# Two heads in one matmul of 128 rows in the recurrent levels of a hybrid decoder trunk

## The reference

```
logf = logaddexp(log(lb), log1p(-lb) + log_sigmoid(f));  k = -expm1(logf);  q = silu(q_raw)
b = cumsum(logf)                                   # along the tokens of a chunk
attn[t, s] = sum_c q[t, c] * exp(b[t, c] - b[s, c]) * k[s, c]     for s <= t
o = attn @ v + (q * exp(b)) @ state
```

## Time and profile before

| | |
|---|---|
| median of three runs | 2279.16 us (2278.46 to 2280.85) |
| profiled execution, its own time | 2280.71 us |
| its span | 2278.9 us |
| PE, DVE, ACT, POOL busy | 94%, 65%, 44%, 17% |
| mean granted TensorE clock | 0.983 of 2.4 GHz |
| levels stage, layer 1 | 164.5 to 280.5 us |
| levels stage, layer 2 | 1287.3 to 1402.7 us |

### The profile page before, as it was taken

The page is one execution under the profiler, slowest core; times in us unless marked ns, Lnnn a source line. Parts: engine busy times, 40 slices in busy tenths (PEclk is TensorE's granted clock), DMA queues, the critical chain, the costliest instruction groups (busy, mean ns, idle before and its releaser), DMA issues.

```text
span 2278.9 us, 32746 instructions
## 1 busy us (share of the span) xinstructions
PE 2146.6 (94%) x12051; PEld 1714.9 (75%) x12051; DVE 1486.5 (65%) x2695; ACT 1009.7 (44%) x1867; POOL 377.5 (17%) x346
## 2 busy tenths in 40 slices
PE   7999999999899998999999999999998989999996
PEld 4897788777677786777579878887866878777774
DVE  4637776654667876777656486766265678377775
ACT  4523334543465335555434233345344643345552
POOL 2002200000000341344300121000000014124441
PEclk9999999999999999999999999999999999999998
DMA  9322333331225675776542223423222266546753
GB/s 309 93 86 61 94 101 93 103 92 51 80 78 175 243 245 226 284 250 247 190 153 85 76 79 93 130 79 93 79 61 79 79 226 241 201 167 247 256 211 119
DMA packets 196573, 333.71 MB, mean 146 GB/s; under 512 B 30528, under 2 KB 153280, under 8 KB 180416
## 3 DMA queue, kind: packets, MB, share of 16 engines
q1 hardware_dynamic: 169184, 305.33, 39.6%
q0 software_dynamic: 19296, 19.98, 2.8%
q10 hardware_dynamic: 7936, 6.30, 0.8%
HBM read 352.48 MB, written 51.38 MB: 177 GB/s over the span
## 4 chain that ended last, share of the span: by engine, by line
PE 73%; DVE 13%; ACT 6%; issue 3%; DMA 3%; POOL 0%; SPq 0%; POOLq 0%; ACTq 0%; DVEq 0%
PE ps L874 68%; PE ps L872 5%; DVE spare L2077 2%; DVE ring_rounded L2095 2%; ACT WH_rounded L1587 2%; DVE nmax L2323 1%; DVE ssq L2262 1%; DMA SQKV<-gate_logits 1%; DMA DVt<-gate_logits 1%; DVE ps L2320 1%; DMA Y<-y_rows 1%; DVE DQK L2264 0%; DVE SC L2693 0%; ACT SC L1723 0%; POOL M L3035 0%
## 5 line engine op out<-in xcount | busy, mean ns | idle before, releaser
L874 PE MATMUL ps<-X_rounded,WH_rounded 128*128 128x512 f32 x768 | 343.8, 448 | 20.9 <-ACT CM L1635 6.5
L2095 DVE TENSOR_TENSOR ring_rounded<-ring,WH_rounded 128x512 fp32r<-128x512 f32 (+2 forms) x190 | 234.9, 1245 | 134.7 <-ACT WH_rounded L1587 134.3
L874 PE MATMUL ps<-H_rounded,WH_rounded 128*128 128x512 f32 x768 | 304.4, 396 | 8.9 <-DVE SC L2693 8.9
L874 PE MATMUL ps<-X_rounded,ring_rounded 128*128 128x512 f32 x768 | 304.3, 396 | 0.0
L874 PE MATMUL ps<-WH_rounded,X_rounded 128*128 128x256 f32 (+1 forms) x960 | 275.1, 287 | 3.1 <-ACT M L1868 1.0
L874 PE MATMUL ps<-ring_rounded,X_rounded 128*128 128x256 f32 (+1 forms) x960 | 271.5, 283 | 0.0
L874 PE MATMUL ps<-WH_rounded,H_rounded 128*128 128x256 f32 (+1 forms) x960 | 271.4, 283 | 0.0
L3035 POOL TENSOR_TENSOR M<-M,SC 128x512 f32<-128x512 f32 x48 | 75.8, 1591 | 997.9 <-DVE SC L2693 997.9
L1587 ACT ACTIVATE WH_rounded<-ring 128x512 fp32r<-128x512 f32 (+2 forms) x190 | 195.2, 1037 | 70.6 <-PE ps L874 62.3
L874 PEld LDWEIGHTS ps<-X_rounded,WH_rounded 128*128 128x128 f32 x768 | 146.7, 191 | 76.4 <-issue 30.4
L874 PEld LDWEIGHTS ps<-WH_rounded,X_rounded 128*128 128x128 f32 x960 | 184.8, 192 | 5.3 <-issue 2.4
(11 more groups left out here) (399 smaller groups left out, 4503.5 us busy)
## 6 DMA issues: line engine op xcount, KB each, us to landing
ring<-in_w_in SPq DMA_DIRECT2D x272, 256.0 KB, 3.9
Y<-in_moe_w_down SPq DMA_DIRECT2D x18, 1024.0 KB, 6.6
ring<-in_ada_w SPq DMA_DIRECT2D x64, 256.0 KB, 4.7
ring<-in_w_branch SPq DMA_DIRECT2D x64, 256.0 KB, 5.4
TM<-in_ada_w SPq DMA_DIRECT2D x14, 1024.0 KB, 10.2
DQK<-in_ada_w SPq DMA_DIRECT2D x14, 1024.0 KB, 9.4
ring<-in_moe_w_down SPq DMA_DIRECT2D x14, 1024.0 KB, 6.4
gate_logits<-CM SPq DMA_DIRECT2D x44, 256.0 KB, 2.9
```

The source lines that it names most:

```text
L874: ins = nc.tensor.matmul(o, lhsT, rhs, start=start, stop=stop)
L2095: ins = v.tensor_tensor(low[j][:, at:at + size], ring[:, j, at:at + size], high[i][:, at:at + size].bitcast(F32), ALU.subtract)
```

## The change

At levels 1 to 7 both heads go through one matmul. The queries are laid out for each token block as two groups of 64 columns, one a head, with zeros in the other head's 64 partitions. A matmul then takes 128 rows and 128 columns, four instead of eight a level, and writes both heads into one PSUM bank (4 or 1, by the level's parity).

The zeros come out of the exponentials: ACT writes the query factors into a new buffer `hgEq` (in DVt, cleared once a layer), each head's partitions into its own group of columns. The one exponential over 128 x 512 becomes three: the early half (128 x 256, with scale -1), and the late half once for each head (64 x 256). POOL multiplies the whole late half of the queries by each of the two groups: two multiplications of 128 x 256 instead of one, and `qs_ready` counts two. On DVE `decay` is one difference over all 512 columns instead of two over 256, and `keep` one predicated copy of 512 columns instead of two of 256. Level 0, step 8, the key product and the order of the queues stay.

```diff
@@ TensorE, levels
-                        eng.wait_ge(qs_ready[i], p.next(qs_ready[i]))
+                        eng.wait_ge(qs_ready[i], p.next(qs_ready[i], 2))
                         eng.wait_ge(ks_ready[i], p.next(ks_ready[i]))
+                        b = level_bank(lv)
+                        free(b)
+                        for c in range(NT):
+                            ins = mm(level_out(b)[:, :, c], hgKs[i][:, tt(c)], hgQs[i][:, c], last=c == 3)
+                        ins.then_inc(filled[b], p.gives(filled[b]))
-                                ins = mm(ps[:, b, c * HD:(c + 1) * HD], k[r, tt(c)], half(q[r, tt(c)], lv, 1), last=last)
@@ ACT
-                            act(hgE[i], hgE[i], ACT.Exp).then_inc(e_ready[i], p.gives(e_ready[i]))
+                                keys_of, late = (half(hgE[i], j, side) for side in range(2))
+                                act(keys_of, keys_of, ACT.Exp, scale=-1.0)
+                                for side in range(2):
+                                    r = slice(side * HD, (side + 1) * HD)
+                                    ins = act(hgEq[i][r, :, side].rearrange("p c (n h) -> p c n h", h=1 << j >> 1),
+                                              late[r].rearrange("p (c n) h -> p c n h", c=NT), ACT.Exp)
+                                ins.then_inc(e_ready[i], p.gives(e_ready[i]))
@@ DVE, decay and keep
-                    v.tensor_tensor(half(hgE[i], j, 0), ref, first, ALU.subtract)
-                    v.tensor_tensor(half(hgE[i], j, 1), second, ref, ALU.subtract).then_inc(
+                    v.tensor_tensor(hgE[i].rearrange("p (n s) -> p n s", s=size), spans, ref, ALU.subtract).then_inc(
...
+                    both = DQK[:, pr % 2, :].rearrange("p (c n a h) -> p c n a h", c=2 * NT, a=2, h=h)[:, :, :, 1]
+                    v.copy_predicated(both, mask.unsqueeze(1).to_broadcast([P, 2 * NT, n, h]),
+                                      ps[:, b, :].rearrange("p (c n h) -> p c n h", c=2 * NT, h=h)).then_inc(
@@ POOL
-                            eng.tensor_tensor(half(hgQs[i], j, 1), half(hgQ[:, pr], j, 1), half(hgE[i], j, 1), ALU.mult).then_inc(
-                                qs_ready[i], p.gives(qs_ready[i]))
+                            late = half(hgQ[:, pr], j, 1).rearrange("p (c n) h -> p c n h", c=NT)
+                            for side in range(2):
+                                to, by = (x[:, :, side].rearrange("p c (n h) -> p c n h", h=h) for x in (hgQs[i], hgEq[i]))
+                                eng.tensor_tensor(to, late, by, ALU.mult).then_inc(qs_ready[i], p.gives(qs_ready[i]))
@@ DVE, once a layer
-                v.memset(flat(Y[:, 0, 2:4]), 0.0).then_inc(vector_step, p.gives(vector_step))
+                v.memset(flat(DVt[:, 0:2]), 0.0).then_inc(vector_step, p.gives(vector_step))
```

More of the change, by code:

```diff
@@ L469, in half, with level_bank, level_out @@
             return ap.rearrange("p (n a h) -> p n a h", a=2, h=1 << j >> 1)[:, :, a]
+        def level_bank(lv):
+            return 4 if lv % 2 else 1
+        def level_out(b):
+            return ps[:, b, :].rearrange("p (a c d) -> p a c d", a=2, c=NT)
         def pick(ap, i):
@@ L480, in build @@
         hgE = [Y[:, 0, i] for i in range(2)]
-        hgQs = [Y[:, 0, 2 + i] for i in range(2)]
+        hgQs = [Y[:, 0, 2 + i].rearrange("p (c a d) -> p c a d", c=NT, a=2) for i in range(2)]
+        hgEq = [DVt[:, i].rearrange("p (c a d) -> p c a d", c=NT, a=2) for i in range(2)]
         hgKs = [Y[:, 1, i] for i in range(2)]
@@ L1045, in levels @@
                         i = (9 * pr + lv) % 2
-                        eng.wait_ge(qs_ready[i], p.next(qs_ready[i]))
+                        eng.wait_ge(qs_ready[i], p.next(qs_ready[i], 2))
                         eng.wait_ge(ks_ready[i], p.next(ks_ready[i]))
-                        q, k = hgQs[i], hgKs[i]
-                    else:
[L1050 to L1053, removed]
+                        b = level_bank(lv)
[3 more added lines that the diff above has]
+                        ins.then_inc(filled[b], p.gives(filled[b]))
+                        p.mark(emptied[b])
+                    else:
                         for hp in range(2):
[L1055 to L1058, removed]
-                                ins = mm(ps[:, b, c * HD:(c + 1) * HD], k[r, tt(c)], half(q[r, tt(c)], lv, 1), last=last)
[L1060 to L1064, removed]
+                            free(hp)
+                        for c in range(NT):
+                            for hp in range(2):
+                                r = slice(hp * HD, (hp + 1) * HD)
+                                ins = mm(ps[:, hp, tt(c)], hgK[r, pr, tt(c)], hgQ[r, pr, tt(c)], last=c == 3)
+                                if c == 3:
+                                    ins.then_inc(filled[hp], p.gives(filled[hp]))
+                                    p.mark(emptied[hp])
                     if lv:
@@ L1892, in _ @@
                             eng.wait_ge(d_ready[i], p.next(d_ready[i]))
-                            act(hgE[i], hgE[i], ACT.Exp).then_inc(e_ready[i], p.gives(e_ready[i]))
+                            if j:
+                                keys_of, late = (half(hgE[i], j, side) for side in range(2))
[5 more added lines that the diff above has]
+                                ins.then_inc(e_ready[i], p.gives(e_ready[i]))
+                            else:
+                                act(hgE[i], hgE[i], ACT.Exp).then_inc(e_ready[i], p.gives(e_ready[i]))
                             p.mark(ks_ready[i])
                             if j:
-                                p.mark(qs_ready[i])
+                                p.mark(qs_ready[i], 2)
                         else:
@@ L2574, in decay @@
                     size = 1 << j
-                    first, second = (half(hgB[:, pr], j, a) for a in range(2))
-                    ref = first[:, :, size // 2 - 1:size // 2].to_broadcast([P, S // size, size // 2])
-                    v.tensor_tensor(half(hgE[i], j, 0), ref, first, ALU.subtract)
-                    v.tensor_tensor(half(hgE[i], j, 1), second, ref, ALU.subtract).then_inc(
+                    spans = hgB[:, pr].rearrange("p (n s) -> p n s", s=size)
+                    ref = spans[:, :, size // 2 - 1:size // 2].to_broadcast([P, S // size, size])
+                    v.tensor_tensor(hgE[i].rearrange("p (n s) -> p n s", s=size), spans, ref, ALU.subtract).then_inc(
                         d_ready[i], p.gives(d_ready[i]))
@@ L2586, in keep @@
                         p.mark(attn_used[pr % 2])
-                    for hp in range(2):
-                        b = (lv % 2) * 4 + hp
-                        eng.wait_ge(filled[b], p.next(filled[b]))
-                        alone()
[L2591 to L2603, removed]
+                        for hp in range(2):
+                            eng.wait_ge(filled[hp], p.next(filled[hp]))
+                            alone()
+                            v.copy_predicated(attnT[pr % 2][hp], repeat(ident[:, :].bitcast(I32), NT), bank3(hp, NT, P)).then_inc(
+                                emptied[hp], p.gives(emptied[hp]))
+                        return
+                    b = level_bank(lv)
+                    eng.wait_ge(filled[b], p.next(filled[b]))
+                    alone()
+                    for before in ((0, 1) if lv == 1 else (level_bank(lv - 1),)):
+                        eng.wait_ge(emptied[before], p.given(emptied[before]))
+                        alone()
+                    mask = half(lmask[:, lv - 1], lv, 1).bitcast(I32)
+                    n, h = mask.shape[1:]
+                    both = DQK[:, pr % 2, :].rearrange("p (c n a h) -> p c n a h", c=2 * NT, a=2, h=h)[:, :, :, 1]
+                    v.copy_predicated(both, mask.unsqueeze(1).to_broadcast([P, 2 * NT, n, h]),
+                                      ps[:, b, :].rearrange("p (c n h) -> p c n h", c=2 * NT, h=h)).then_inc(
+                        emptied[b], p.gives(emptied[b]))
                 low_at = strewn(1)
```

3 lines of the change are left out of this document (2 added, 1 removed).

## The result

The changed kernel takes 2293.03 us (median of six runs, 2287.23 to 2296.7), the kernel before 2281.68 (six runs beside it, 2278.46 to 2284.1). The ratio is 1.0049, 95% interval 1.0032 to 1.0066: slower by half a per cent. The forecast was 2282.3 with a range of 2270 to 2291, and "within 0.2%" as the likeliest case. It was wrong, and the time is outside the range.

The account below looks back on a forecast made before the run. TensorE's queue in the two levels stages was taken as the bound. Savings and waits came to +0.15 us a layer, +1.5 with split delays, +3.1 for both layers; on the median 2279.2 that gave 2282.3, range 2270 to 2291.

Parts of the forecast that it names:

- TensorE's part: TensorE between levels: a level takes 0.90 us instead of 1.04, and plain intervals shorten by 0.25 each.
- Rival (4): 128-row matmuls are no shorter: a level takes 1.12 us instead of 0.90, +4.0 a layer, 2290.3; chance 0.10.
- the price of the way behind the copies: Six intervals behind gate copies: TensorE waits for the longer way through ACT and POOL, +4.41 us a layer before split delays.
- the other four copies cost nothing: Gate copies n = 11, 20, 14 and 23: other waits cover them or their single instructions stay, so no cost.
- case B: Copies n = 5 and 17: split waits for level n+1, 3.88 us against 3.30, +0.58 each; n = 29 likewise, +1.09.
- Case A: Copies n = 2, 8 and 26: the way through ACT and POOL takes 4.02 us instead of TensorE's 3.30, +0.72 each.
- the slip: DVE's 0.69 us weight split comes between POOL's two multiplications at n = 2, 5, 26, 29; half counted, +1.38 a layer.
- P: Theory in the follow-up experiments: GpSimd's added product and VectorE's work hold each other up wherever they meet.
- Q: Follow-up theory: exponentials queue behind ScalarE's gate copy, query products behind those; added work lengthens that way, hardly mattering elsewhere.
- (3): Slower: the split delays POOL's pair every time and its second multiplication takes 0.98 us, +4.4 a layer, 2288.0; chance 0.24.
- (2): Faster: products come earlier than forecast and TensorE stays the bound, -4.4 us a layer, 2270.4; chance 0.24.
- (5): New gaps of up to 1.1 us lower TensorE's clock, ending above 2284; chance 0.04.

Follow-up runs that it names:

- before_order: The kernel before, with ScalarE doing the next level's exponentials ahead of a gate copy instead of behind it: 2277.03 us, ratio 0.999.
- one_product: The changed kernel without GpSimd's second query product, the second head's queries left as zeros: 2278.7 us, ratio 1.0000.
- static_zeros: The changed kernel with zeros kept in the query buffer, one exponential, two differences and two GpSimd products of 64 partitions: 2285.86 us, ratio 1.0025.

## Why the prediction was wrong, step by step

**TensorE's part: right in kind, too small.** Forecast 0.90 for a level, measured 0.81; forecast 3.05 and 2.36 for the intervals, measured 2.95 and 2.26. Rival (4) fell: with 0.81 against 1.04 us the matmuls of 128 rows are shorter than twice as many of 64 side by side. By the rule of the Trainium skill (TensorE: Matmul & The Clock Gate, Part 3, "Packing small matmuls"), as I applied it to the heads, nothing would have been saved; here the measurement decides. What stays is a gain of 0.10 a level more than I had, and with it -1.05 us a layer that I did not count (-4.72 instead of -3.67 over the table's rows of the nine plain intervals and of those through the KdT product, through the outputs and from level 0 to 1).

**VectorE: no cover was lost, but less was saved.** It is busy for 90.4 us of the stage, as before. One predicated copy has a mean of 0.89 instead of the 0.74 that I took for two of 0.53, one difference 0.81 instead of 0.69 for two of 0.50. At the plain intervals that stays hidden, as forecast.

**The step that failed is the price of the way behind the copies, and "the other four copies cost nothing".** The mechanism was the forecast one: ScalarE's queue behind the copy, GpSimd's behind that, TensorE waiting for the second product. Its terms were too small: the six intervals grew by 7.87 us a layer where I had 4.41 + 1.38 = 5.79, and n = 20 by 1.01 where I had nothing. For n = 5 (case B) I had 0.54 + 0.54 + 0.94 + 0.05 + 1.76 + 0.05 = 3.88; it took 4.77. The rows for it, in the changed kernel: ScalarE, then VectorE, then the chain of waits (start, length, what):

```profile
185.38 0.63 ACT L1595 ACTIVATE WH_rounded<-ring 128x512 fp32r<-128x512 f32 x1 [1.46 <-PE ps L883]
185.91 0.40 ACT L1903 ACTIVATE Y<-Y 128x256 f32<-128x256 f32 x1
186.22 0.83 ACT L1906 ACTIVATE DVt<-Y 64x256 f32<-64x256 f32 x2
```

```profile
187.08 0.43 DVE L2634 TENSOR_TENSOR Y<-Y 128x256 f32<-128x256 f32 x1 [1.82 <-ACT DVt L1906]
187.43 0.74 DVE L2618 COPY_PREDICATED DQK<-lmask,ps 128x512 f32<-128x512 int32 x1
188.06 0.67 DVE L2112 TENSOR_TENSOR ring_rounded<-ring,WH_rounded 128x512 fp32r<-128x512 f32 x1
```

```profile
187.13 2.20 POOL Y L3040 x2
189.32 0.04 issue
```

The split starts 0.78 us after level n+1 (184.60 to 185.38; I had 0.54), then 0.53, the three exponentials 1.14 (185.91 to 187.05; I had 0.94), 0.08, the two products 2.19 (I had 1.76), 0.05. Together 4.77. So of the miss of 0.89, 0.24 is the split's start (why it comes later was not traced), 0.20 the exponentials, 0.43 the products and 0.03 the signal. Case A came out nearer: n = 2 of layer 1, without a slip, took 4.14 where I had 4.02.

The exponentials were mis-sized where I wrote that 64 partitions count as no saving. They are a loss: the overlap of 0.10 that follows another exponential of the full width is missing between the two.

The products hold the slip that I gave half a chance each. The pair took 1.66 us at n = 2 in layer 1 and 2.17 to 2.20 at n = 5 and 26 there, and at n = 2 in layer 2:

```profile
175.38 1.66 POOL Y L3040 x2
...
264.84 2.17 POOL Y L3040 x2
...
1306.64 2.17 POOL Y L3040 x2
```

At n = 2 of layer 1 VectorE's split started only at 176.56, too late to come between. At n = 5 it stands at 188.06, right behind the copy of 187.43 and in the middle of the pair. The same interval was 4.14 in layer 1 and 4.64 in layer 2 (1304.21 to 1308.85), which is the price of one slip, 0.50. At n = 29 too the pair took 2.18. So the slip came seven times of the eight, at 0.50 instead of 0.69: 1.75 us a layer instead of 1.38. Without it the pair's 1.66 is even less than my 1.76. What is left of the miss lies in the exponentials (0.20 at each of six) and in the split's start (0.24 at the three of case B). The Trainium skill (SBUF — State Buffer, "SBUF: two separate sides") states that GpSimd and a VectorE instruction with two SBUF inputs take a shared port in turn, each for a whole instruction. The trace agrees: with the split (0.67 us) behind the copy the pair is 0.50 us longer, and without it, at n = 2 of layer 1, it is not.

**Copy n = 20** is where P has a share of its own. I counted it as covered by level 6's wait. The chain of VectorE that level 6 waits for, in the changed kernel:

```profile
240.88 1.22 DVE L2654 SCALAR_TENSOR_TENSOR DQK<-DQK,edec,ps 64x64 f32<-64x64 f32 x4
242.13 1.15 DVE L2112 TENSOR_TENSOR ring_rounded<-ring,WH_rounded 128x512 fp32r<-128x512 f32 x1
243.20 1.20 DVE L2594 TENSOR_TENSOR Y<-M 128x512 f32<-128x512 f32 x1
244.33 0.41 DVE L2634 TENSOR_TENSOR Y<-Y 128x256 f32<-128x256 f32 x1
```

```profile
241.99 1.87 POOL Y L3040 x2
243.87 0.97 issue
```

and in the kernel before:

```profile
241.58 0.69 DVE L2095 TENSOR_TENSOR ring_rounded<-ring,WH_rounded 128x512 fp32r<-128x512 f32 x1
...
242.86 0.42 DVE L2617 TENSOR_TENSOR Y<-Y 128x256 f32<-128x256 f32 x1
```

There GpSimd's single product ran from 240.79 to 241.53, ahead of the split. Now the exponentials behind the copy end at 241.91, the pair of products runs from 241.99 to 243.86, and the split and the difference take 1.15 and 1.20 us; on their own they take 0.69 and 0.67. From the split's start to the keys it is 2.20 us (242.13 to 244.33) instead of 1.28 (241.58 to 242.86): 0.92 of the 1.01 us that the interval grew. With the exponentials ahead it is back to 3.77. It is P's hold-up, but Q's order put it there.

**The rivals.** (3) was the nearest: the slips came, and the products were longer. Its sum, 2288.0, still had 0.94 for exponentials that took 1.13, and nothing for n = 20. (2) was the wrong sign because the way behind the copies was the bound at all six. (5), the clock: the gap of 2.33 us ahead of level 7 of pair 3 is in both layers. In this execution the clock fell behind it in layer 1 alone:

```profile
278.00:280.00 2.00, 1.28 (x10) 1.26 (x11) 0.08 (x1) 0.59 (x2) 1.90 (x2) 1.00 0.74 254
280.00:282.00 2.00, 2.00 (x9) 1.42 (x7) 1.86 (x3) 0.00 (x0) 0.00 (x0) 0.53 0.00 0
282.00:284.00 2.00, 2.00 (x11) 2.00 (x11) 0.04 (x1) 0.00 (x0) 0.00 (x0) 0.50 0.04 8
```

There the pair's outputs, at 1.2 GHz, repeat at 1.28 us instead of 0.67 (281.95 to 283.23). In layer 2 the clock stayed at 1.00 to 1412. It lies behind the stretch that is compared, so it is no part of the +8.3. The rest of the layer, from level 7 of pair 3 to the next layer's level 0, took 1012.2 us before and 1017.0 in the changed kernel, but 1016.1 in before_order, and 1010.9 to 1017.8 over the nine profiled executions, whose code is nearly the same there. So one execution can't tell whether the change adds to it.

**What stays open.** Ratio and stages agree within the interval for six of the eight changed versions. For one_product the stages say -4.4 us and the ratio 0.0 (up to 3 either way), for static_zeros +1.6 against +2.7 to +8.7. These differences outside the stages were not explained. The forecast's 2282.3 and the measured 2293.03 are 10.7 us apart. Of these, 2.5 are its base (2279.2 for the median before, which over six runs is 2281.7), 4.9 the two stages (+8.3 instead of 2 x 1.70), and some 3.3 lie outside the stages and have no cause shown.

## What to carry to other kernels

Before adding work to an engine, look at what that engine's queue waits for just before: here an instruction that waits for TensorE stood ahead of exponentials that had been ready for 2.25 us when they began, and what was added behind it came out at TensorE, at six to seven places a stage. A change that loses in such a place may gain once the queue is reordered: the same edit is worth +8.3 us in one order and -10.8 in the other (208.22 against 219.04 in the two stages). If the slack of a way is 0.4 us, add up its terms from rows of the very shape (partitions too), and count each partner that shares its port as arriving in between.

## What the runs showed of the hardware

- An exponential of 256 columns lasts 0.41 us on 128 and on 64 partitions. Behind one another, two of 128 partitions start 0.31 apart, two of 64 on different halves 0.41 to 0.42.
- A GpSimd product of 256 columns takes 0.71 us at the shortest on 64 partitions and 0.72 on 128, and two on different halves take as long as two full ones (2.20 for the pair behind n = 5 in static_zeros, 2.19 in the changed kernel). The Trainium skill (GPSIMD Engine Reference, section 2.1, "Instruction dispatch") says that each core works on its own 16 partitions of every instruction. That half of the partitions leaves cores idle instead of saving time is my inference from it, and the equal times agree.
- Eight float32 matmuls of 128 rows and 128 columns, each with its weights, take 0.81 us before the next gate matmul; the sixteen of 64 rows and 64 columns that they replace, two row halves side by side, take 1.04.
